# Moving the first branch's merge products into the attentions, and six more early gate units, in a two-block layer on one Trainium2 core

## The chip, the cores and the metric

The kernel runs on one core of a Trainium2 chip. The metric is the device time of one execution in microseconds. Before the change the median of three runs is 2440.82 us (2437.47 to 2442.12). The engines are TensorE (PE, its weight loads PEld), VectorE (DVE), ScalarE (ACT), GpSimd (POOL) and SyncE (SP), which here only issues transfers.

## What is computed

Two blocks over 512 tokens of width 1024, in float32. The first is attention and convolution with a mixture of experts (`peer_ffn`); the second has three branches that are gated and merged:

```python
h = rms_norm(x, norm_g)
p = h @ w_in
y_a = rwkv7_mix(...) * silu(z_a)                      # a recurrence over the tokens
y_b = sliding_window_sink_attn(q, k, v, pos, ...) * silu(z_b)   # q, k normalised, then rope
y_c = memory_cross_attn(xq, mem, ...) * silu(z_c)
gates = sigmoid(p_gate).reshape(b, t, 3, 1024)
merged = gates[..., 0, :] * (y_a @ w_proj_a) + gates[..., 1, :] * (y_b @ w_proj_b) \
       + gates[..., 2, :] * (y_c @ w_proj_c)
x = x + merged @ w_out
```

`rope` turns pairs that lie 32 apart in each head of 64: out = u * cos + crossed(u) * sin, where crossed(u) exchanges the two halves of 32 and changes one's sign. In the expert layer each token picks 16 of 16384 experts for each of 8 heads, by the best sums of two score lists; it takes a dot product with each picked row of `peer_u`, then adds up the picked rows of `peer_v` by weight.

## The kernel before

Activations of the projections lie transposed, with 128 channels on the partitions and the 512 tokens along the free dimension. All weights come in one stream of **units** of 128 x 1024 floats (512 KB) through a ring of four (`Weights`, L172). A product is made of three matmuls on parts rounded to fp32r (`product`, L165: high by high at L167, high by low at L168, low by high at L169); ScalarE makes the high part of each unit (`high_part`, L221 and L225, two buffers, made for unit u + 2 once TensorE finished unit u, `finished`, L229), GpSimd the low part (`low_parts`, L242), and VectorE does it in the expert stage (`low_part`, L250). The order of the units is `UNITS` (L68).

Much projection work is independent of what runs at its time and is laid beside other work by a **Filler** (L275): each `fill.pe(pe, n)` emits n steps on TensorE, ScalarE copies a finished unit to `stage` (L349), and SyncE stores it in `z_store` (L353). The second filler does the 46 units of `fill2`, each 128 channels of a projection: four for the gate of the recurrence, ten for the sliding attention (q, k, v and its gate), eight for the memory attention, and 24 for the sigmoid gates of the merge. A *whole* step is one `product` of 512 columns (three matmuls), eight to a unit.

**Early units.** 40 of the 46 units (`EARLY`, L67) are computed for their first 384 tokens beside the experts, in `merge_and_experts` (L1158), before the last 128 tokens exist. `early_steps` (L1108) spreads their steps, with those of 13 units for the recurrence, over the groups `Z_FROM` to `Z_UNTIL` (L1094 and L1095), that is 204 to 254. These steps have 384 columns, eight to a unit. SyncE loads each unit and stores 384 tokens of it. Later the filler makes only the last 128 tokens of these units, as a *short* step: two plain float32 matmuls at L320, four steps to a unit (`PART_STEPS`). Steps by stage before: 46 in `rwkv_prepare`, 89 in `rwkv_core`, 3 + 8 + 6 in `finish_branches`, 38 in `sliding_attention`, up to 21 in `memory_attention`. In all there are 40 x 4 + 6 x 8 = 208, so the last 30 of the sliding attention and 18 of the memory attention are whole ones.

**Experts.** A group is two picks of one head for a tile of 128 tokens: GpSimd issues two gathers (L1602), each 128 rows of 2048 floats (1 MB); VectorE makes the dot products (L1921), ScalarE the gelu (L1549) and the scaled diagonals (L1556), and TensorE adds the weighted rows with them (L2182). The four tiles come one after another. At its start, SyncE loads the rows of w_out (`raw_out`, a ring of four) and the query weights (`raw_query`, a ring of three) in plain float32 for the first tile: TensorE multiplies at L2137 (output product), then at L2082 (queries). The normalised tiles 1 to 3 of h2 lie over `raw_query`; VectorE writes them in the order 2, 3, 1 (`REST`, L998) by `scale` (L1838 to L1844), each waiting for the queries that read the slot beneath it: {1: 10, 2: 8, 3: 9}.

**finish_branches** (L3027) normalises y_a by head, gates it, normalises and turns q and k. q and k come back from `z_store` as `swz` in one transfer (L2995). Five matmuls by a signed permutation with the gain multiplied in (`swap`, L3055 to L3061) give crossed(u) in PSUM; `rotate` (L3144) on VectorE multiplies it by the sine (L3148), the straight part by gain and cosine (L3150), and adds (L3154). TensorE's order by hand: sums of y, swap 0 and 1, sums of squares of y, sums of squares of q and k (L2208), swap 2 and 3, three fill steps, spreads (L2217), sums for the memory queries, swap 4, v turned (L3093), eight fill steps, spreads, six fill steps. After it follow the two attentions (`attention`, L433) with fill steps in each iteration.

**merge_second** (L3257) runs twelve products, three branches for each of four pairs of output rows. Product n has 8 steps (4 for each of two rows), goes to bank pair n % 2 and waits for the gating of n - 2. SyncE loads the gates (512 KB for each n); ScalarE makes the sigmoid (L3313), VectorE multiplies bank by gate (L3356), adds the second and third branch to the first (L3361), and after the third splits the sum in high and low (L977 and L979). Eight units of w_out follow.

## Time and profile before

| | busy us | share of the span |
|---|---|---|
| profiled execution | 2434.74 (own time) | span 2432.9 |
| TensorE | 2159.3 | 89% |
| TensorE weight loads | 1445.3 | 59% |
| VectorE | 1762.3 | 72% |
| ScalarE | 852.9 | 35% |
| GpSimd | 701.1 | 29% |
| transfers | 713.53 MB, 293 GB/s mean | gathers 53.4% of 16 engines |

The stages lie so: first block up to about 450 us, the output product and the experts from 450 to 1933 us (first gathers at 497), recurrence 1933 to 2169, finishing the branches 2169 to 2219, sliding attention 2219 to 2276, memory attention 2277 to 2311, merge 2315 to 2384, the last product to the end. Durations in a timeline are those of one instruction or of a run of equal ones (x8: eight records; a plain float32 matmul has two records). "idle before <-" says how long the engine stood and who released it. The lower of TensorE's two clocks (1.2 GHz of 2.4) is a granted share of 0.50. A stage average says little about what ends last in it; the rows below are of single stages.

### The profile page before, as it was taken

How to read it: one execution, taken by the hardware profiler on the slowest of the kernel's cores; microseconds unless marked ns; L12 is line 12 of the kernel's file. 1: busy time of each engine (PE TensorE's matmuls, PEld its weight loads, DVE VectorE, ACT ScalarE, POOL GpSimd, SP SyncE). 2: the span in 40 equal slices, each digit the busy share in tenths (PEclk: the TensorE clock that was granted, in tenths of full speed). 3: DMA queues.
4: the chain of work that ended last, by engine and by line, in shares of the span. 5: the costliest groups of instructions: out<-in, count | busy, mean ns of one | idle time of the engine just before them, and what ended most of it. 6: DMA issues, size and time to landing. Idle time of an engine off the chain costs nothing. (4 is left out here: it accounts for less than half of the span.)

```text
span 2432.9 us, 34962 instructions
## 1 busy us (share of the span) xinstructions
PE 2159.3 (89%) x12602; PEld 1445.3 (59%) x12602; DVE 1762.3 (72%) x3986; ACT 852.9 (35%) x1969; POOL 701.1 (29%) x574
## 2 busy tenths in 40 slices
PE   8999899998999898877777888799999899888999
PEld 6887566664444444423233333377777788876777
DVE  7999696587666766677777767789887685456663
ACT  4222664143323323232333233333333332225631
POOL 0000312364333333334343333443334100001133
PEclk9999999999999999999999999999999999988999
DMA  4333214499999999999999999999999852342152
GB/s 155 104 104 113 75 52 154 176 377 415 421 413 421 419 418 416 413 417 400 421 419 420 417 413 409 411 404 418 421 421 421 318 170 82 117 160 82 60 187 95
DMA packets 137210, 713.53 MB, mean 293 GB/s; under 512 B 14672, under 2 KB 25296, under 8 KB 71248
## 3 DMA queue, kind: packets, MB, share of 16 engines
q0 software_dynamic: 73728, 536.90, 53.4%
q1 hardware_dynamic: 63312, 174.41, 20.0%
q8 instruction: 101, 1.65, 0.3%
q14 instruction: 69, 0.57, 0.1%
HBM read 689.76 MB, written 21.50 MB: 292 GB/s over the span
## 5 line engine op out<-in xcount | busy, mean ns | idle before, releaser
L2182 PE MATMUL bank<-peer_uv,peer_diag 128*128 128x512 f32 x1844 | 869.5, 614 | 202.1 <-ACT peer_diag L1556 200.8
L1921 DVE SCALAR_TENSOR_TENSOR peer_uv<-peer_uv,h 128x1024 f32<-128x1024 f32 x512 | 619.2, 1220 | 345.7 <-DMA peer_uv<-in_peer_uv,peer_index 345.3
L1602 POOL DMA_INDIRECT peer_uv<-in_peer_uv,peer_index x512 | 554.2, 1082 | 846.5 <-PE bank L2182 581.4
L2182 PEld LDWEIGHTS bank<-peer_uv,peer_diag 128*128 128x128 f32 x1844 | 338.6, 194 | 641.4 <-issue 640.6
L169 PE MATMUL bank<-hT_high,weight_low 128*128 128x384 f32 (+1 forms) x952 | 345.8, 363 | 0.0
L167 PE MATMUL bank<-hT_high,weight_high 128*128 128x512 f32 (+1 forms) x744 | 322.5, 434 | 5.6 <-POOL weight_low L250 2.3
L242 POOL TENSOR_TENSOR weight_low<-weight_ring,weight_high 128x1024 fp32r<-128x1024 f32 x46 | 112.1, 2437 | 611.2 <-ACT weight_high L225 611.2
L1549 ACT ACTIVATE peer_gelu<-peer_dots 128x2 f32<-128x2 f32 (+1 forms) x257 | 52.2, 203 | 644.9 <-DVE peer_uv L1921 644.5
L168 PE MATMUL bank<-hT_low,weight_high 128*128 128x512 f32 (+1 forms) x744 | 275.0, 370 | 0.0
L225 ACT ACTIVATE weight_high<-weight_ring 128x1024 fp32r<-128x1024 f32 x145 | 153.1, 1056 | 298.2 <-PE bank L169 271.9
L1556 ACT ACTIVATE peer_diag<-const,peer_weight 128x128 f32<-128x128 f32 x461 | 162.8, 395 | 234.0 <-DVE peer_weight L1717 233.7
L169 PEld LDWEIGHTS bank<-hT_high,weight_low 128*128 128x128 f32 x952 | 179.4, 188 | 18.2
L167 PEld LDWEIGHTS bank<-hT_high,weight_high 128*128 128x128 f32 x744 | 140.8, 189 | 48.7 <-issue 27.8
L168 PEld LDWEIGHTS bank<-hT_low,weight_high 128*128 128x128 f32 x744 | 140.9, 189 | 40.7 <-issue 25.6
L250 DVE TENSOR_TENSOR weight_low<-weight_ring,weight_high 128x1024 fp32r<-128x1024 f32 x89 | 108.6, 1220 | 10.1 <-ACT weight_high L225 10.1
L250 POOL TENSOR_TENSOR weight_low<-weight_ring,weight_high 128x1024 fp32r<-128x1024 f32 x10 | 34.3, 3434 | 261.8 <-ACT weight_high L225 261.7
L320 PE MATMUL bank<-last_h,weight_ring 128*128 128x128 f32 x640 | 89.6, 296 | 3.2 <-ACT fill_stage L349 3.2
L925 DVE SCALAR_TENSOR_TENSOR convT_whole<-z_u,cols,convT_whole 128x512 f32<-128x512 f32 x120 | 90.0, 750 | 0.0
L320 PEld LDWEIGHTS bank<-last_h,weight_ring 128*128 128x128 f32 x640 | 82.4, 207 | 9.2 <-issue 6.9
L925 DVE SCALAR_TENSOR_TENSOR z_odd<-z_u,cols,z_odd 128x512 f32<-128x512 f32 x112 | 84.0, 750 | 0.0
L167 PE MATMUL bank<-hT_high,early_high 128*128 128x384 f32 x208 | 79.8, 384 | 0.0
L168 PE MATMUL bank<-hT_low,early_high 128*128 128x384 f32 x208 | 70.4, 339 | 0.0
(469 smaller groups left out, 3160.7 us busy)
## 6 DMA issues: line engine op xcount, KB each, us to landing
weight_ring<-in_weights SPq DMA_DIRECT2D x224, 512.0 KB, 4.2
peer_uv<-in_peer_uv,peer_index POOLq DMA_INDIRECT x512, 10.5
z_store<-fill_stage SPq DMA_DIRECT2D x30, 256.0 KB, 2.4
z_store<-early_stage SPq DMA_DIRECT2D x40, 192.0 KB, 13.2
merge_z<-z_store SPq DMA_DIRECT2D x8, 768.0 KB, 6.6
merge_z<-z_store SPq DMA_DIRECT2D x12, 512.0 KB, 4.5
raw_query<-in_weights SPq DMA_DIRECT2D x10, 512.0 KB, 5.3
raw_out<-in_weights SPq DMA_DIRECT2D x8, 512.0 KB, 7.4
```

The costliest lines, as they stand in the source:

```text
L167: nc.tensor.matmul(to, left[0], right[0], start=start, stop=False)
L168: nc.tensor.matmul(to, left[0], right[1], start=False, stop=False)
L169: return nc.tensor.matmul(to, left[1], right[0], start=False, stop=stop)
L225: self.nc.scalar.activation(self.high_at(u).bitcast(F32R), self.ring[:, u % RING], ACT.Copy).then_inc(self.high_ready, 1)
L242: self.nc.gpsimd.tensor_tensor(self.low[:, slot].bitcast(F32R), self.ring[:, slot], self.high_at(u), ALU.subtract).then_inc(self.split, 1)
L250: vector.tensor_tensor(self.low[:, u % RING].bitcast(F32R), self.ring[:, u % RING], self.high_at(u), ALU.subtract).then_inc(self.split, 1)
L320: mm = self.nc.tensor.matmul(to, self.ring[:, f], self.last[:, f], start=f == 0, stop=f == DT - 1)
L925: nc.vector.scalar_tensor_tensor(to, u[:, c, k:k + T], cols("conv_w", k * DT + c), to, ALU.mult, ALU.add).then_inc(tap_done, 1)
L1556: nc.scalar.activation(diag[:, p % SLOTS], ident, ACT.Copy, scale=weight[:, p % TOPK:p % TOPK + 1]).then_inc(diag_ready, 1)
L1602: pool.indirect_dma_start(uv[:, p % SLOTS], None, peer_uv, bass.IndirectOffsetOnAxis(index[:, n % 2, p % TOPK:p % TOPK + 1], 0)).then_inc( ...
L1921: nc.vector.scalar_tensor_tensor(uv[:, p % SLOTS, 0:D], uv[:, p % SLOTS, 0:D], 1.0, h2[:, t], ALU.mult, ALU.mult, accum_out=dots[:, p % TO ...
L2182: mm = nc.tensor.matmul(bank[2 * t + c][:], diag[:, p % SLOTS], uv[:, p % SLOTS, D + c * 512:D + (c + 1) * 512], start=(n == first_of(t) a ...
```

## The change

1. `EARLY` is 46: all units of `fill2` have their first 384 tokens made beside the experts. The steps in the 50 groups grow from 408 to 456, and two low parts can fall into one group (`while lows`).
2. The products of the first branch (four of the twelve of the merge) become eight **half units** of the second filler: four whole steps each, two to a weight unit. They are stored ungated in rows 46 to 53 of `z_store`. The filler has 46 x 4 + 8 x 4 = 216 steps; 11 are left for the start of the merge. `merge_second` has 8 products, reloads the first branch (`first`, two buffers, 512 KB each) and gates it from SBUF. ScalarE's and SyncE's orders follow.
3. The swap products go. Four transfers of 32 partitions x 5 x 2 KB, issued behind that of `swz`, load the rows with the halves of 32 exchanged, and VectorE multiplies them by a signed gain and by the sine. Fill steps in the finish are 3 + 4 + 4.
4. `raw_out` has six slots, of which two lie in slots 0 and 1 of `raw_query`. The loads go in the order raw_out 4, 5, query 0, raw_out 6, 7, query 1, 2; the queries move one slot on, and `scale` waits for {1: 8, 2: 9, 3: 10}.

```diff
-EARLY = 40
+EARLY = 46
@@ Filler
-            self.begins.append(self.begins[-1] + (PART_STEPS if n < part else DT))
+            self.begins.append(self.begins[-1] + (PART_STEPS if n < part else DT if n < whole else DT // 2))
...
+            else:
+                e = (n - self.whole) % 2
+                mm = product(self.nc, to, self.ring[:, DT // 2 * e + k], self.items[n][0][:, k], k == 0, k == DT // 2 - 1)
+                if e == 0 and k == DT // 2 - 1:
+                    mm.then_inc(self.half_done, 1)
+                ends = e == 1 and k == DT // 2 - 1
@@ merge_and_experts, SyncE
                 w.load(sp, ub + RING)
                 sp.wait_ge(w.done, ub)
-                for m in range(3):
+                for k in (4, 5):
+                    raw_out_load(k)
+                raw_query_load(0)
+                for k in (6, 7):
+                    raw_out_load(k)
+                for m in (1, 2):
                     raw_query_load(m)
-                for k in range(4, DT):
-                    raw_out_load(k)
@@ merge_and_experts, VectorE
-                        dve.wait_ge(raw_query_done, {1: 10, 2: 8, 3: 9}[t])
+                        dve.wait_ge(raw_query_done, {1: 8, 2: 9, 3: 10}[t])
...
-                    if lows < LOWS_BESIDE and low_group(lows) <= g:
+                    while lows < LOWS_BESIDE and low_group(lows) <= g:
@@ second_block
-                  lambda n: first_unit("fill2") + n, [(hT, ACT.Copy, 1.0)] * FILL2, z_store, EARLY, places[1])
+                  lambda n: first_unit("fill2") + n if n < FILL2 else first_unit("merge") + (n - FILL2) // 2,
+                  [(hT, ACT.Copy, 1.0)] * FILL2 + [None] * (2 * FIRST_MERGED), z_store, EARLY,
+                  places[1], FILL2)
@@ rwkv_core, SyncE
                 sp.dma_start(late.swz[:], fill.store[4:14].rearrange("n p t -> p n t")).then_inc(swz_arrived, 16)
+                for o in range(0, P, 32):
+                    o2 = o + 32 if o % HD == 0 else o - 32
+                    sp.dma_start(late.crossed_z[o:o + 32], fill.store[4:9, o2:o2 + 32].rearrange("n p t -> p n t")
+                                 ).then_inc(crossed_arrived, 16)
@@ finish_branches, TensorE
-                pe.wait_ge(swz_arrived, 16)
-                swap(0)
-                swap(1)
...
-                swap(2)
-                swap(3)
                 fill.pe(pe, 3)
...
-                swap(4)
-                pe.wait_ge(crossed_ready, 4)
+                pe.wait_ge(swz_arrived, 16)
...
-                fill.pe(pe, 8)
+                fill.pe(pe, 4)
...
-                fill.pe(pe, 6)
+                fill.pe(pe, 4)
@@ finish_branches, VectorE
-                    nc.vector.tensor_tensor(crossed[:, i % 2], bank[4 + i % 2][:], sin, ALU.mult).then_inc(crossed_ready, 1)
+                    nc.vector.scalar_tensor_tensor(crossed[:, i % 2], late.crossed_z[:, i], late.cross_gain[:, i // 4:i // 4 + 1], sin,
+                                                   ALU.mult, ALU.mult).then_inc(crossed_ready, 1)
@@ merge_second
+    products = 12 - FIRST_MERGED
+    place = lambda m: 3 * (m // 2) + 1 + m % 2
...
-                fill.pe(pe, DT * FILL2)
-                for n in range(12):
-                    ring = w.wait(pe, u0 + n)
-                    if n >= 2:
-                        pe.wait_ge(parts, 2 * (n - 1))
+                fill.pe(pe, DT * fill.limit)
+                for m in range(products):
+                    ring = w.wait(pe, u0 + m)
+                    if m >= 2:
+                        pe.wait_ge(parts, 2 * (place(m - 2) + 1))
...
-                    if n >= 2:
-                        w.finished(act, u0 + n - 2)
+                    if n >= 4 and n % 3:
+                        w.finished(act, u0 + n - n // 3 - 3)
...
-                        nc.vector.tensor_tensor(to, bank[2 * (n % 2) + e][:], gate[:, n % 2, e], ALU.mult
+                        of = bank[2 * ((n - n // 3 - 1) % 2) + e][:] if n % 3 else first[:, n // 3 % 2, e]
+                        nc.vector.tensor_tensor(to, of, gate[:, n % 2, e], ALU.mult
```

## Rows read from the trace of the kernel before

**Rows 1.** Busy time by stage: stretch, length, five engines, granted clock, transfer share, GB/s.

```profile
1620.00:1680.00 60.00, 58.23 (x272) 47.58 (x271) 53.80 (x113) 21.98 (x42) 23.52 (x19) 1.00 1.02 419
...
2219.00:2276.00 57.00, 54.86 (x354) 38.21 (x354) 41.86 (x168) 41.30 (x129) 12.02 (x5) 0.94 0.25 84
...
2315.00:2384.00 69.00, 68.91 (x289) 55.57 (x290) 43.48 (x48) 25.70 (x24) 26.43 (x11) 0.98 0.51 176
```

**Rows 2.** DMA issues, 1600 to 1900 us: tensors, queue, count, KB each, us to landing.

```profile
z_store<-early_stage SPq DMA_DIRECT2D x33, 192.0 KB, 13.5
```

**Rows 3.** Timeline of TensorE, 1888 to 1898 us: start, duration, engine, line, operation, idle before.

```profile
1890.22 1.95 PE L2182 MATMUL bank<-peer_uv,peer_diag 128*128 128x512 f32 x4 [0.49 <-ACT peer_diag L1556]
...
1891.61 0.74 PE L167 MATMUL bank<-hT_high,early_high 128*128 128x384 f32 x1
...
1896.89 1.52 PE L2182 MATMUL bank<-peer_uv,peer_diag 128*128 128x512 f32 x3 [0.50 <-ACT peer_diag L1556]
```

**Rows 4.** Waits between 1600 and 1900 us: who waits for whom, us, times, longest.

```profile
DVE peer_uv L1921 <- DMA peer_uv<-in_peer_uv,peer_index: 45.9, 39, 2.8
```

**Rows 5.** Timelines of TensorE and SyncE's queue around 455 us.

```profile
453.32 7.03 PE L2137 MATMUL bank<-raw_out,merged_whole 128*128 128x512 f32 x16
...
463.94 8.83 PE L2137 MATMUL bank<-raw_out,merged_whole 128*128 128x512 f32 x16 [3.59 <-DMA raw_out<-in_weights]
...
455.31 5.40 SPq L1282 DMA_DIRECT2D raw_out<-in_weights  x4
```

**Rows 6.** Timelines of VectorE and GpSimd, 540 to 552 us.

```profile
540.12 1.28 DVE L1843 SCALAR_TENSOR_TENSOR h<-x,peer_rstd,rows 128x1024 f32<-128x1024 f32 x1
...
546.19 1.28 DVE L1843 SCALAR_TENSOR_TENSOR h<-x,peer_rstd,rows 128x1024 f32<-128x1024 f32 x1 [1.16 <-PE bank L2082]
...
551.64 1.63 POOL L1602 DMA_INDIRECT peer_uv<-in_peer_uv,peer_index  x1 [4.77 <-PE bank L2182]
```

**Rows 7.** Timeline of TensorE in the finish of the branches, 2166 to 2219 us.

```profile
2176.22 1.98 PE L3060 MATMUL bank<-swz,swap_gains 128*128 128x512 f32 x4 [1.70 <-DMA swz<-z_store]
...
2189.85 3.76 PE L3060 MATMUL bank<-swz,swap_gains 128*128 128x512 f32 x4
...
2204.80 3.27 PE L320 MATMUL bank<-last_h,weight_ring 128*128 128x128 f32 x24
```

**Rows 8.** Timeline of VectorE in the same stretch.

```profile
2190.03 0.20 DVE L3179 TENSOR_SCALAR finish_ms<-bank 128x40 f32<-128x40 f32 x1 [7.48 <-PE bank L2208]
```

**Rows 9.** Timeline of TensorE in the sliding attention, 2238 to 2242 us.

```profile
2238.72 0.70 PE L471 MATMUL bank<-swz 64*128 64x256 f32 x4
...
2240.35 0.48 PE L167 MATMUL bank<-hT_high,weight_high 128*128 128x512 f32 x1
...
2241.90 0.70 PE L471 MATMUL bank<-swz 64*128 64x256 f32 x4
```

**Rows 10.** Timelines of VectorE, ScalarE and GpSimd in the merge, 2328 to 2340 us.

```profile
2328.09 1.29 DVE L3356 TENSOR_TENSOR merge_part<-bank,merge_gate 128x512 f32<-128x512 f32 x2 [4.31 <-PE bank L169]
...
2329.30 3.42 DVE L3361 TENSOR_TENSOR merged2T_whole<-merged2T_whole,merge_part 128x512 f32<-128x512 f32 x2
...
2333.69 1.29 DVE L3356 TENSOR_TENSOR merge_part<-bank,merge_gate 128x512 f32<-128x512 f32 x2 [0.97 <-PE bank L169]
...
2338.24 0.41 DVE L977 CAST merged2T_high<-merged2T_whole 128x512 fp32r<-128x512 f32 x1
...
2338.69 0.69 DVE L979 TENSOR_TENSOR merged2T_low<-merged2T_whole,merged2T_high 128x512 fp32r<-128x512 f32 x1
...
2328.02 1.06 ACT L225 ACTIVATE weight_high<-weight_ring 128x1024 fp32r<-128x1024 f32 x1 [3.08 <-PE bank L169]
...
2329.16 2.41 POOL L242 TENSOR_TENSOR weight_low<-weight_ring,weight_high 128x1024 fp32r<-128x1024 f32 x1 [3.20 <-ACT weight_high L225]
```

**Rows 11.** The page's DMA issues, columns as in group 2.

```profile
z_store<-fill_stage SPq DMA_DIRECT2D x30, 256.0 KB, 2.4
...
merge_z<-z_store SPq DMA_DIRECT2D x12, 512.0 KB, 4.5
```

More of the change, by code:

```diff
@@ L3431, in constants @@
     halves = (p // 64 == c // 64)
[L3433 to L3438 removed]
+    sign = np.where(np.arange(P) % 64 < 32, -1.0, 1.0).astype(np.float32)[:, None]
     s2 = np.arange(2 * P)[None, :]
```

131 lines of the change are left out of this document (75 added, 56 removed).

## The prediction

> **What bounds the kernel now.** I read the busy time by stage first [rows 1]. Three kinds of stage matter here. In the experts, of which 1620 to 1680 us is a sample, the transfers run at a share of 1.02 and 419 GB/s while TensorE is busy 58.23 of 60 us: the DMA engines are full and TensorE is almost full too. The waits name the tighter one: VectorE stood 39 times for the expert rows, 45.9 us in all [rows 4], and TensorE's wait at a group of picks is 0.50 us [rows 3]. The groups repeat every 1896.89 - 1890.22 = 6.67 us [rows 3]. From 2166 us on the transfers are mostly light: finishing the branches (from 2166 to 2219), the sliding attention (57 us, TensorE busy 54.86) and the merge (69 us, busy 68.91) [rows 1] go by TensorE and by the chains that feed it. So a microsecond of TensorE is worth a microsecond in the merge and nearly that in the attention, a part of one in the finish, and nothing in the experts until it passes the transfers there.
>
> **1. Start of the experts.** Today eight matmuls' worth of output product waits 3.59 us for raw_out at 463.94, because the four last loads are issued at 455.31, after three query loads [rows 5]. With six slots two of the four go out first, and the two behind a single query load. The stall goes: 3.6 us, and up to 5.1 if the matmuls behind it, which take 8.83 us instead of 7.03 at the lower clock that follows the stall [rows 5], also recover 1.4 to 1.5. I take -5, since the loads are the only thing named; low end -3.6. What is late next is the merged input, which is ready in time for the first half.
>
> **2. The changed waits of scale.** scale(2) waits today for 8 queries and started at 540.12 without a wait; scale(3), which waits for 9, started at 546.19 after 1.16 us on TensorE [rows 6]. Now scale(2) waits for the ninth, so it moves to about 546.1, 6.0 us later. Queued behind it on VectorE are two dot products of a running group (1.22 us each) and the picks after them; who waits for those is TensorE, and behind it the gather on GpSimd, here the one at 551.64, itself after 4.77 us of waiting [rows 6]. Nothing in these rows is idle by itself, so of the 6.0 us some 4 reach the gathers, less what the one wait takes out of the next (1.16) and TensorE's own wait. I take +4, ends 0 and +6. A loss here shifts everything in the experts, as later groups are bound by transfers and do not catch up.
>
> **3. Six more early units in the experts.** Each loads 512 KB and stores 192 KB, a row of 384 tokens [rows 2]: 6 x (524,288 + 196,608) bytes = 4.33 MB. At the row's 419 GB/s [rows 1] that is 10.3 us if transfers stay the bound. TensorE gets 48 steps more in 50 groups, 0.96 a group, each of three 384-column matmuls; from 1891.61 to 1896.89, less the 0.50 of waiting, TensorE makes 24 of them and then has the next group, hence about 0.18 us each after the first and 0.5 us a group more [rows 3]. A group then needs 1896.89 - 1890.22 - 0.50 + 0.5 = 6.67 us of TensorE if its wait vanishes, against 6.67 + 0.206 = 6.88 us of transfers: the transfers still win, by 3%. But in 1620 to 1680 TensorE is at 58.23, and 9 groups x 0.5 makes 62.7 us against 61.9 of transfers; two resources that close do not overlap perfectly. I take +12, ends +9 and +20. The six low parts fall to VectorE, 1.2 us each, inside its 1.2 us waits for rows [rows 4].
>
> **4. Finishing the branches.** The five swap products go: two in 1.98 us, two in 3.76 us, which is the granted clock at 1.2 instead of 2.4 GHz, and the fifth in about 1.98 at that lower clock, 7.7 us of TensorE, and so does TensorE's wait of 1.70 us for swz [rows 7], since the first use of swz is now the sums of squares. Six fill steps leave: a step is 4 records, 24 of them take 3.27 [rows 7], so 6 x 0.545 = 3.3 us. Sum 12.7 us of TensorE. What is late next: the crossed loads, four of 0.33 MB issued behind swz (1.31 MB, 3.1 us at 419 GB/s), so VectorE begins the rotations nearer 2179.5 than 2177.4 and the mem and xqz loads behind them land 3 us later. VectorE had 7.48 us of waiting on the sums of squares [rows 8], which takes this. Following the order of TensorE and VectorE through, I end the stage about 2207 to 2208 instead of 2218: -10, ends -6 and -12.7. The two gain operations on [128, 1] and four more issues on SyncE's queue cost nothing, they lie in the scan, whose SyncE has no load due then.
>
> **5. The sliding attention.** Its iteration lasts 2241.90 - 2238.72 = 3.18 us [rows 9] and holds two whole fill steps, six 512-column matmuls, 1.55 us from 2240.35 to 2241.90 [rows 9]. All of its 38 steps are short ones now (4 x 46 = 184 short steps, of which 46 + 89 + 11 lie before), so these two become 8 records, 1.05 to 1.1 us [rows 7]: 0.47 us less in 15 iterations, 7 us, and 1.0 us of a wait for a low part goes. VectorE is busy 41.86 of 57 us [rows 1] and the row-by-row chain of maximum, exponential and sum takes over somewhere, so -6.5, ends -3 and -9.
>
> **6. The memory attention** has 21 whole steps instead of 18, over the same 0.70 us each, the three more in iterations that stood partly idle: +0.5, ends 0 and +2.
>
> **7. The merge.** Before: 12 products, each 5.60 us (2333.69 - 2328.09 between their first readers [rows 10]), 68.5 us with the slow first ones. After: 11 steps of fill (7.7 us, 9.1 with the low clock at the start), then 8 products, 44.8: TensorE alone would end at 53.9. But the first branch must be stored (2.4 us for 256 KB) and reloaded (4.5 us for 512 KB) [rows 11] after the last fill: 9.1 + about 1 + 2.4 + 4.5 + 1 of issue = 18. VectorE per pair of outputs: three gatings of 1.29, two additions of 3.42, two splits of 1.1, together 12.9 [rows 10], against 11.2 of TensorE. And the high part of the next weights stands on ScalarE behind the gate of two places on, then 1.06 and 2.41 us on GpSimd [rows 10]. Stepping through these: the third product starts at 25.8, the fifth at 39.0, the seventh at 51.4, and the eighth ends at 62.6. So -5.9; I take -5.5, ends -14.7 (TensorE alone) and 0.
>
> **Sum.** -5 + 4 + 12 - 10 - 6.5 + 0.5 - 5.5 = -10.5 us. The profiled execution took 2434.74, so 2424.2; the median of the three runs lies 6.1 us above it, so 2430.3 on the scale of the median. A measurement of this kernel can tell some 0.2% (4.9 us) from no change.
>
> **A rule that speaks against it.** The additions that read two operands from SBUF take 3.42 us for two, 1.71 each, the gatings that read PSUM and SBUF 0.65 each; GpSimd's low part of 2.41 us begins just before the additions [rows 10]. The eight gatings of the first branch will read two operands from SBUF as well. At 0.65 each step 7 stands; at 1.71 each they take 8 x 1.06 = 8.5 us more, which is rival B. The Trainium skill, "SBUF — State Buffer", section "Who interferes with whom", has a rule for it: a VectorE instruction with two SBUF inputs contends with a GpSimd instruction that reads SBUF, and whoever comes second waits for the whole of the other. The trace agrees with it in these rows. By the rule it costs only where a low part is under way when the gating comes; by my stepping-through the low parts end 2 us or more before, which is why it isn't the forecast.
>
> **Rivals.**
> A, slower: the experts become bound by TensorE's own order. Place: a group between Z_FROM and Z_UNTIL. TensorE's wait for peer_diag (0.50 us) is not slack but a loop from picks to weights, and stays; then a group lasts 6.67 + 0.5 = 7.17 to 7.25 us, 50 x 0.5 to 0.6 = 25 to 30 us instead of 12. For it: TensorE is at 58.23 of 60. Against it: VectorE's waits for rows, 45.9 us. It decides the sign from 7.2 us a group on: +27 there makes +5 in the sum. Time 2443 to 2450; I say 2448. Chance 0.12.
> B, within the measurement: the eight gatings of the first branch take 1.71 us as the additions do, 2.1 us more on VectorE in each pair; three pairs lie before the last product, so it ends at 62.6 + 6.3 = 68.9 and the merge lasts as before (+5.5); and the finish, with TensorE idle more often, spends its 9.7 us of sums and products at 1.2 GHz as the swap at 2189.85 does [rows 7], so that it gives only 5 (+5). Time 2441. Chance 0.16.
> C, the loads are hidden and TensorE is the only bound behind the experts: -12.7 - 9 - 14.7, with +9 for the experts and -5 at the start, is about -28: 2412 to 2416. Against it: the 18 us that the first branch needs in the merge. Chance 0.14.
> D, the change does only half: crossed loads come so late (they need the fill store's rows and SyncE) that the rotations set the finish. Then -4 instead of -10: 2436. Chance 0.10. The rest, 0.48, is the forecast with its own range of 2422 to 2439.
>
> **Chances.** Faster by over 0.2% (below 2435.9): 0.42 of the forecast's 0.48, 0.14 of C, 0.05 of D, 0.02 of B: 0.63. Within: 0.06 + 0.05 + 0.13 + 0.03 (A) = 0.27. Slower (above 2445.7): 0.09 of A, 0.01 of B: 0.10. The range goes from 2416 (C) to 2446, which leaves out half of A and half of C.
>
> **What the profile after would show.** Step 1: no wait for raw_out near 464. Step 2: a VectorE wait of about 6 us at 540 minus 5. Step 3: 6.9 us between gathers, share still 1.02; at 7.2 A holds. Step 4: no line for swap, about 43 us of stage. Step 5: iterations of 2.7 us. Step 7: TensorE idle up to 5 us ahead of every second product, waiting for a low part of GpSimd or for a gating, and eight first gatings of 0.65 us (B: 1.7). The prediction is wrong if groups of the experts pass 7.2 us, or if the three stages behind together give less than 10 us.

## The result and the profile after

Over 20 runs each, the changed kernel takes 2443.89 us (2438.94 to 2452.66) and the kernel before 2438.40 us; the ratio is 1.0031 with a 95% interval of 1.0021 to 1.0040 (two slow runs of the kernel before, 2665.53 and 3520.37 us, are left out of it). It is slower by 5.5 us by the medians and 7.6 us by the ratio, a small difference but clear of no change, where 10.5 us less were forecast. The two profiled executions lie 8.9 us apart (spans 2441.8 and 2432.9).

Where it went, read from the two traces. The first column runs from the first matmul of the output product to the first gather. The second and the third both start at that gather and run to those of group 10 and of group 206, so the third holds the second; the fourth runs from group 206 to 254 (48 groups). Then come the finish, from the last matmul of the scan (the recurrence) to the first of the sliding attention, that attention, the memory attention, and the merge, from its end to the first product with w_out:

| us | start | to g10 | to g206 | 206 to 254 | finish | sliding | memory | merge | span |
|---|---|---|---|---|---|---|---|---|---|
| before | 43.4 | 58.5 | 1085.4 | 314.9 | 49.9 | 58.0 | 34.9 | 72.0 | 2432.9 |
| after | 37.8 | 65.1 | 1091.1 | 340.1 | 48.2 | 51.6 | 35.1 | 68.0 | 2441.8 |
| forecast of the change | -5 | +4 | +4 | +12 | -10 | -6.5 | +0.5 | -5.5 | -10.5 |

Without the second column, which the third holds, these changes add up to +13.4 us against -10.5 forecast. The largest misses are the fourth column (13.2 us) and the finish (8.3 us). What is left (the first block, the scan) is the same code and still moved by up to 5 us between traces, so small differences are taken from repeated runs below.

The windows that answer to [rows 1] (start and end, length, five engines, granted clock, transfer share, GB/s):

```profile
1620.00:1680.00 60.00, 60.00 (x288) 50.74 (x287) 54.81 (x111) 23.02 (x44) 22.44 (x19) 1.00 1.01 414
...
1800.00:1860.00 60.00, 50.93 (x225) 41.05 (x226) 47.42 (x84) 21.21 (x40) 22.00 (x16) 0.93 0.96 382
...
2240.00:2289.00 49.00, 44.27 (x375) 33.81 (x373) 39.93 (x162) 34.59 (x123) 2.35 (x1) 0.99 0.36 114
...
2327.00:2392.00 65.00, 54.81 (x225) 42.86 (x225) 36.78 (x48) 24.21 (x25) 22.11 (x9) 0.95 0.62 219
```

TensorE is full in the first of them, then at 50.93 of 60 us, while the transfers fall to a share of 0.96 and 382 GB/s: neither is the bound there. The 48 groups as a whole, before and after:

```profile
1582.13:1897.04 314.91, 293.92 (x1346) 236.27 (x1347) 265.24 (x506) 113.13 (x216) 120.48 (x97) 1.00 1.01 417
```

```profile
1579.04:1919.14 340.10, 315.78 (x1470) 263.43 (x1471) 272.73 (x513) 119.72 (x228) 125.95 (x96) 0.97 1.00 400
```

The share of the transfer engines hardly moves (1.01 to 1.00), but the rate falls from 417 to 400 GB/s: a full share alone does not show that the stage moves its bytes as fast as before. The waits between 1600 and 1940 us say who stood. Before, VectorE stood for the low part of a weight unit for 2.6 us in all; after:

```profile
DVE weight_low L251 <- ACT weight_high L226: 33.0, 14, 5.4
...
DVE peer_uv L1947 <- DMA peer_uv<-in_peer_uv,peer_index: 23.3, 21, 2.4
...
DVE weight_low L251 <- ACT early_high L226: 11.7, 7, 6.5
```

One of these waits, in order of cause. SyncE issues the load of a unit at 1839.27; ScalarE, which splits the units in the order of their loads, gets it only at 1852.13; VectorE stands 5.45 us ahead of the low part at 1853.22; behind that stand its picks, so TensorE's diagonals and the next gathers come late:

```profile
1839.27 0.33 SPq L212 DMA_DIRECT2D weight_ring<-in_weights  x1
...
1852.13 1.06 ACT L226 ACTIVATE weight_high<-weight_ring 128x1024 fp32r<-128x1024 f32 x1 [3.17 <-DMA weight_ring<-in_weights]
...
1853.22 1.23 DVE L251 TENSOR_TENSOR weight_low<-weight_ring,weight_high 128x1024 fp32r<-128x1024 f32 x1 [5.45 <-ACT weight_high L226]
...
1856.36 3.75 PE L2208 MATMUL bank<-peer_uv,peer_diag 128*128 128x512 f32 x4 [4.24 <-ACT peer_diag L1582]
...
1856.42 1.31 POOL L1628 DMA_INDIRECT peer_uv<-in_peer_uv,peer_index  x1 [10.12 <-DVE x L1753]
```

GpSimd stood 10.12 us before it could issue, where 3 to 4 us are usual. What such a pause costs the transfers shows in the lower rate above.

At the start of the experts (TensorE, then VectorE and GpSimd, answering to [rows 5] and [rows 6]):

```profile
450.10 7.03 PE L2163 MATMUL bank<-raw_out,merged_whole 128*128 128x512 f32 x16
...
456.96 3.60 PE L2163 MATMUL bank<-raw_query,merged_whole 128*128 128x512 f32 x8
...
460.40 3.60 PE L2163 MATMUL bank<-raw_out,merged_whole 128*128 128x512 f32 x8
...
538.78 1.28 DVE L1869 SCALAR_TENSOR_TENSOR h<-x,peer_rstd,rows 128x1024 f32<-128x1024 f32 x1 [7.88 <-PE bank L2108]
...
487.94 1.09 POOL L1628 DMA_INDIRECT peer_uv<-in_peer_uv,peer_index  x1 [2.99 <-DVE peer_index L1722]
...
549.58 1.10 POOL L1628 DMA_INDIRECT peer_uv<-in_peer_uv,peer_index  x1 [10.19 <-PE bank L2208]
```

The stall of 3.59 us is gone. scale(2) now waits 7.88 us for the ninth query. The gather of group 9, which came 54.92 us after the first before (551.64 - 496.72), comes 61.64 us after it (549.58 - 487.94).

In the finish of the branches, answering to [rows 7], first the row of the kernel before that has the stage's first matmuls, then SyncE, TensorE and VectorE after:

```profile
2170.85 3.67 PE L3064 MATMUL bank<-yaT,const 128*128 128x512 f32 x8 [0.81 <-PEq L2546]
```


```profile
2188.20 0.38 SPq L3024 DMA_DIRECT2D swz<-z_store  x1
...
2188.62 4.26 SPq L3027 DMA_DIRECT2D crossed_z<-z_store  x4
...
2194.35 6.63 PE L3091 MATMUL bank<-yaT,const 128*128 128x512 f32 x8 [3.84 <-PEq L2575]
...
2201.76 13.77 PE L2234 MATMUL bank<-const,finish_sq 128*128 128x2 f32 x72 [0.78 <-DVE yaT L3180]
...
2206.65 0.75 DVE L3169 SCALAR_TENSOR_TENSOR crossed<-crossed_z,cross_gains,sincos 128x512 f32<-128x512 f32 x1 [4.94 <-DMA crossed_z<-z_store]
```

and the windows from 2190 to 2203:

```profile
2190.00:2197.00 7.00, 3.16 (x8) 1.49 (x7) 2.11 (x5) 0.92 (x3) 0.00 (x0) 0.75 0.98 360
...
2198.00:2203.00 5.00, 4.22 (x16) 2.14 (x15) 2.08 (x3) 2.52 (x5) 0.00 (x0) 0.77 1.07 207
```

SyncE issues the four crossed loads in 4.26 us, the larger swz in 0.38. The barrier between the blocks waits for it: TensorE's gap is 3.84 us instead of 0.81, and its first eight records take 6.63 us at 1.2 GHz where they took 3.67. From 2198 to 2203 the crossed loads are what is under way (nearly all bytes move in pieces of 2 KB, the length of their rows, and swz has landed by 2200.5): the transfer engines are busy (share 1.07), the rate is 207 GB/s, where it had been 360 with swz.

In the merge (VectorE's first gating, additions and casts, two of each; TensorE's three waits), answering to [rows 10]:

```profile
2345.86 1.29 DVE L3396 TENSOR_TENSOR merged2T_whole<-merge_first,merge_gate 128x512 f32<-128x512 f32 x2 [19.46 <-DMA merge_first<-z_store]
...
2348.28 1.28 DVE L3401 TENSOR_TENSOR merged2T_whole<-merged2T_whole,merge_part 128x512 f32<-128x512 f32 x2
...
2351.88 2.57 DVE L992 CAST merged2T_high<-merged2T_whole 128x512 fp32r<-128x512 f32 x1
...
2369.58 0.42 DVE L992 CAST merged2T_high<-merged2T_whole 128x512 fp32r<-128x512 f32 x1
...
2393.63 3.43 DVE L3401 TENSOR_TENSOR merged2T_whole<-merged2T_whole,merge_part 128x512 f32<-128x512 f32 x2
...
2354.22 0.79 PE L168 MATMUL bank<-ybT_high,weight_high 128*128 128x512 f32 x1 [8.13 <-POOL weight_low L243]
...
2367.48 0.50 PE L168 MATMUL bank<-ybT_high,weight_high 128*128 128x512 f32 x1 [0.40 <-POOL weight_low L243]
...
2380.87 0.50 PE L168 MATMUL bank<-ybT_high,weight_high 128*128 128x512 f32 x1 [1.63 <-POOL weight_low L243]
```

### The profile page after: what moved, and what is told of

Its sections match the earlier page's. It is cut to its first block and busy times, and to the rows that moved or that the text cites. A ratio compares the mean times of both kernels' runs of the same rounds, so it can differ in the third digit from the quotient of the medians.

```text
span 2441.8 us, 35192 instructions
## 1 busy us (share of the span) xinstructions
PE 2153.2 (88%) x12688; PEld 1455.1 (60%) x12688; DVE 1758.6 (72%) x3992; ACT 854.4 (35%) x1983; POOL 686.9 (28%) x568
## 5 line engine op out<-in xcount | busy, mean ns | idle before, releaser
L168 PE MATMUL bank<-hT_high,weight_high 128*128 128x512 f32 (+1 forms) x720 | 306.6, 426 | 4.5 <-POOL weight_low L251 2.3
L243 POOL TENSOR_TENSOR weight_low<-weight_ring,weight_high 128x1024 fp32r<-128x1024 f32 x40 | 98.1, 2454 | 608.9 <-ACT weight_high L226 608.9
L169 PE MATMUL bank<-hT_low,weight_high 128*128 128x512 f32 (+1 forms) x720 | 263.1, 365 | 0.0
L168 PEld LDWEIGHTS bank<-hT_high,weight_high 128*128 128x128 f32 x720 | 135.7, 188 | 45.9 <-issue 25.7
L169 PEld LDWEIGHTS bank<-hT_low,weight_high 128*128 128x128 f32 x720 | 135.7, 188 | 39.2 <-issue 24.9
L251 DVE TENSOR_TENSOR weight_low<-weight_ring,weight_high 128x1024 fp32r<-128x1024 f32 x92 | 112.1, 1219 | 43.4 <-ACT weight_high L226 43.1
L251 POOL TENSOR_TENSOR weight_low<-weight_ring,weight_high 128x1024 fp32r<-128x1024 f32 x10 | 34.3, 3435 | 258.5 <-ACT weight_high L226 258.4
L326 PE MATMUL bank<-last_h,weight_ring 128*128 128x128 f32 x736 | 99.1, 285 | 8.0 <-ACT fill_stage L364 4.5
L326 PEld LDWEIGHTS bank<-last_h,weight_ring 128*128 128x128 f32 x736 | 89.8, 196 | 13.4 <-issue 11.4
L168 PE MATMUL bank<-hT_high,early_high 128*128 128x384 f32 x232 | 90.8, 391 | 0.0
L169 PE MATMUL bank<-hT_low,early_high 128*128 128x384 f32 x232 | 79.3, 342 | 0.0
```

The lines of the kernel that those rows point to most:

```text
L168: nc.tensor.matmul(to, left[0], right[0], start=start, stop=False)
L169: nc.tensor.matmul(to, left[0], right[1], start=False, stop=False)
L243: self.nc.gpsimd.tensor_tensor(self.low[:, slot].bitcast(F32R), self.ring[:, slot], self.high_at(u), ALU.subtract).then_inc(self.split, 1)
L251: vector.tensor_tensor(self.low[:, u % RING].bitcast(F32R), self.ring[:, u % RING], self.high_at(u), ALU.subtract).then_inc(self.split, 1)
L326: mm = self.nc.tensor.matmul(to, self.ring[:, f], self.last[:, f], start=f == 0, stop=f == DT - 1)
```

## The experiments

All times are medians; each ratio is against runs of the kernel before that were taken with it, with its 95% interval. The kernel before itself had medians from 2433.77 to 2438.40 us in these sets, so kernels of different sets are compared by their ratios; "clear" means clear of the two intervals taken together, which is some 4 to 5 us. The stages are of one trace each and are read as in the table above.

| run | ratio to before | interval | to g10 | to g206 | 206 to 254 | finish |
|---|---|---|---|---|---|---|
| e1 loads as changed | 1.0006 | 0.9991 to 1.0021 | 66.0 | 1092.0 | 315.4 | 50.3 |
| e2 loads, old slots | 0.9977 | 0.9961 to 0.9992 | 58.4 | 1084.6 | 317.3 | 50.6 |
| e3 EARLY = 46 | 1.0047 | 1.0029 to 1.0065 | 59.9 | 1085.2 | 336.7 | 53.0 |
| e4 dense, EARLY = 40 | 1.0047 | 1.0027 to 1.0068 | 60.3 | 1087.3 | 324.9 | 52.7 |
| e5 as e3, two matmuls a step | 1.0006 | 0.9993 to 1.0019 | 59.8 | 1085.7 | 336.6 | 51.5 |
| e6 after, crossed loads later | 1.0019 | 1.0006 to 1.0032 | 63.1 | 1087.8 | 337.1 | 42.2 |
| e7 after, swaps kept | 1.0065 | 1.0052 to 1.0079 | 65.9 | 1090.7 | 340.4 | 54.8 |
| e8 after, EARLY = 40 | 1.0015 | 1.0001 to 1.0030 | 65.3 | 1091.1 | 316.1 | 43.0 |
| e9 as e3, splits a group later | 1.0035 | 1.0023 to 1.0048 | 58.3 | 1084.4 | 333.1 | 53.3 |
| e10 EARLY = 43 | 1.0023 | 1.0004 to 1.0041 | 59.9 | 1085.4 | 328.7 | 50.6 |
| e11 after, both repairs | 1.0011 | 1.0000 to 1.0023 | 58.2 | 1084.4 | 336.9 | 43.7 |
| e12 loads and crossed alone | 0.9968 | 0.9954 to 0.9982 | 58.5 | 1085.5 | 314.7 | 45.1 |
| e13 as e3, gathers a group later | 1.0084 | 1.0066 to 1.0102 | 58.6 | 1088.9 | 340.5 | 52.2 |
| e14 before, gathers a group later | 1.0064 | 1.0050 to 1.0077 | 59.8 | 1091.2 | 327.5 | 50.6 |

**The start of the experts: e1 and e2.** e1 is the fourth part of the change alone. e2 differs from it in this:

```diff
-                return raw_query[:, k - 4].rearrange("p k f -> p (k f)")
+                return raw_query[:, k - 3].rearrange("p k f -> p (k f)")
...
-                        dve.wait_ge(raw_query_done, {1: 8, 2: 9, 3: 10}[t])
+                        dve.wait_ge(raw_query_done, {1: 10, 2: 8, 3: 9}[t])
```

and the queries stay in slots m % 3.

> The kernel before with the fourth part of the change alone: six slots for raw_out, the two extra ones over slots 0 and 1 of raw_query, queries one slot on, scale waits {1: 8, 2: 9, 3: 10}. Theory L (the moved wait gives back most of what the earlier loads win): the first gathers start 8.8 us earlier, at 487.9 instead of 496.7; scale(2) then waits some 7 us for the ninth query and at the end of the experts only 3 us are left, so -3 us in all. Rival: the lead that is lost at scale(2) was lost to the other parts of the change; then this kernel is 8 to 9 us faster.

> As the run before, but the extra slots lie over slots 1 and 2 of raw_query, so that the queries keep their slots and scale its waits {1: 10, 2: 8, 3: 9}. Theory L: the 8.8 us of the start are kept through the experts, -8 us or so in all. Rival (the transfers are full from 500 us on, so an earlier start only moves the queue): -3 us, as the run before.

e1 took 2439.58 us, e2 2432.40, the kernel before 2437.83. From product to gather both need 37.9 and 37.8 us instead of 43.4. Every trace with the earlier loads has 37.8 to 38.0 us there, while the kernels without them have 40.5 to 44.1, so the loads are worth 3 to 6 us. The time of e2 is 5.6 us less than before by the ratio (2.0 to 9.5). Moving the waits of scale costs 7.2 us between the two medians, and by group 10 the traces are 7.6 us apart. The waits in question (e1, then e2):

```profile
539.51 1.28 DVE L1853 SCALAR_TENSOR_TENSOR h<-x,peer_rstd,rows 128x1024 f32<-128x1024 f32 x1 [6.19 <-PE bank L2092]
```

```profile
535.05 1.28 DVE L1853 SCALAR_TENSOR_TENSOR h<-x,peer_rstd,rows 128x1024 f32<-128x1024 f32 x1
...
541.12 1.28 DVE L1853 SCALAR_TENSOR_TENSOR h<-x,peer_rstd,rows 128x1024 f32<-128x1024 f32 x1 [0.87 <-PE bank L2092]
```

The rival of e1, that the lead was lost to the other parts of the change, falls: e1 is not faster than the kernel before. The -3 us expected for it was missed too, its interval ends at -2.2. Between theory and rival of e2 (-8 and -3 us) the time does not decide; the traces do: to group 206 e2 needs 1084.6 us from its first gather and the kernel before 1085.4, so full transfers did not swallow the earlier start.

**More early units: e3, e4, e5, e10.** e3 and e10 change `EARLY` alone, e4 the start of the early steps, e5 the step:

```diff
-Z_FROM = FINISH_AT[2] + 12
+Z_FROM = FINISH_AT[2] + 18
@@ e5, on top of EARLY = 46
-                            mm = product(nc, bank[2 + n % 4][:, 0:EARLY_T], ring[:, k], h3T[:, k, 0:EARLY_T], k == 0, k == DT - 1)
+                            to, left, right = bank[2 + n % 4][:, 0:EARLY_T], ring[:, k], h3T[:, k, 0:EARLY_T]
+                            nc.tensor.matmul(to, left[0], right[0], start=k == 0, stop=False)
+                            mm = nc.tensor.matmul(to, left[1], right[0], start=False, stop=k == DT - 1)
```

> The kernel before with EARLY = 46 alone (and the loop over the low parts that it needs). 48 more steps in 50 groups and 4.33 MB more. Theory S (weights arrive after the group in which ScalarE and VectorE are written to split them, and VectorE stands with the picks behind it): the experts last 20 to 25 us longer, with 20 us or more of VectorE waits at the low part, against some 5 us gained in the sliding attention and 4 where whole steps leave the memory attention: +12 to +18 us in all. Theory B (bytes): the experts last 10.3 us longer, and the total is within +0 to +3.

> The kernel before with EARLY = 40 as it was, but Z_FROM six groups later: the same 408 steps and the same bytes in 44 groups, 9.27 steps a group instead of 8.16. Theory B (bytes alone set the time): no change, 0 to +2 us. Theory S: the stalls at the low part appear without one byte more, 10 us or more longer. Theory T (TensorE has no room): a group needs 6.2 + 1.11 x 0.52 = 6.8 us against 6.65 of transfers in 44 groups, +6 us, and no waits at the low part.

> e3 (EARLY = 46 alone) with two matmuls in each early step instead of three: the product with the low part of the activations is left out there, so the gates and the z of the recurrence are less exact. Bytes, loads, their order and the places of the splits stay. A group has 9 x 0.175 = 1.6 us less of TensorE. Theory T (TensorE had no room): the experts come back to the 10.3 us of the bytes, without waits at the low part. Theory S (splits are written for a group in which the weights are not there yet): TensorE ends a unit a little earlier, so some waits go, but more than half of the 33 us of VectorE's waits at the low part stay, and the experts stay 15 us or more longer than before.

> The kernel before with EARLY = 43 alone: 8.64 steps a group, half of the way. Theory S as a threshold (a unit lasts 0.93 group, its successor in the ring is wanted 2.78 groups later): some waits at the low part, 10 to 20 us, and +5 us in all. Theory B: 5 us of bytes in the experts, +0 to +2 in all.

e3 took 2448.94 us, e4 2449.05, e10 2442.27, e5 2439.30. From group 206 to 254, e3 needs 21.8 us more than before, of which the bytes are 10.3 (an estimate, at 419 GB/s); e10 13.8, of which the bytes are 5.2; e4, without one byte more, 10.0. In time, e3 and e4 are both 11.5 us slower than before by the ratios, at the low end of what theory S had for e3 (+12 to +18). The waits at the low part appear in e4 as well as in e3. VectorE's waits from 1600 to 1940 us in e3, in e4 and in e5, and a window of e5:

```profile
DVE weight_low L250 <- ACT weight_high L225: 36.8, 15, 5.4
...
DVE weight_low L250 <- ACT early_high L225: 9.9, 5, 4.5
```

```profile
DVE weight_low L250 <- ACT weight_high L225: 25.6, 10, 5.4
...
DVE weight_low L250 <- ACT early_high L225: 11.7, 8, 5.4
```

```profile
DVE weight_low L250 <- ACT weight_high L225: 24.2, 10, 5.4
```

```profile
1800.00:1860.00 60.00, 42.31 (x164) 29.82 (x162) 45.53 (x82) 20.81 (x39) 20.36 (x16) 0.88 1.01 404
```

e4 falsifies the account by bytes alone. e5 falsifies the lack of room on TensorE: with 42.31 of 60 us busy it needs 336.6 us for the 48 groups, e3 336.7. The expectation for e5 was that some waits go and more than half stay; 26.8 us of 46.7 stayed, without any gain: VectorE waits 39.9 us for rows, in e3 21.7. Its better total is from other stages (from the end of the experts to that of the scan its trace is 7 us shorter) and is not explained. e10 shows that there is no threshold at 9 steps: at 8.64 VectorE already waits 30.7 us at the low part, where 10 to 20 were expected, and the groups cost 8.6 us over the bytes.

**What sets the waits: e9, e13, e14.**

```diff
@@ e9, on top of EARLY = 46
-KEEP_BEHIND = 2
+KEEP_BEHIND = 3
-    return Z_FROM + 1 + e - 2 if e < HIGHS else z_group(e - HIGHS) + 3
+    return Z_FROM + 1 + e - 2 if e < HIGHS else z_group(e - HIGHS) + 4
@@ e13 on top of EARLY = 46, e14 on the kernel before
-                        pool.wait_ge(summed, g - RINGS + 1)
+                        pool.wait_ge(summed, g - RINGS + 1 + (Z_FROM <= g < LAST_GROUP))
```

> e3 (EARLY = 46 alone) with ScalarE keeping unit n and splitting unit n + 4 three groups behind unit n's last step instead of two (KEEP_BEHIND = 3), and VectorE's low part four behind instead of three. Theory S, first form (the group was too early for the transfer, which lands 11 to 13 us after its issue): VectorE's waits at the low part fall from 47 us to under 10, and the kernel is 8 us or more faster than e3. Second form (a ring of four units is the limit: unit n + 4 is wanted by TensorE 2.6 groups after unit n's last step and now gets there after four): VectorE's waits go, TensorE waits for its weights instead, and the time is that of e3 or longer.

> e3 (EARLY = 46 alone) with each gather from group 204 on issued one group later (it waits for one more finished group of TensorE), so that up to 2 MB less stand in the queues in front of a weight load. Theory Q (latency of the weight loads behind the gathers sets the stalls): weights land some 3 to 5 us sooner, VectorE's waits at the low part fall from 47 us to under 20, and the experts get 5 to 10 us shorter than e3's. Theory R (the ring of four units and the order written for the engines): the waits at the low part stay above 35 us, and the kernel is as slow as e3 or slower, since expert rows come later too.

> The same gathers one group later in the kernel before, EARLY = 40: the control. Where the shorter lead costs nothing by itself, no change (within 2 us). If the lead was needed, VectorE's waits for expert rows grow from 50 us and the kernel is 5 us or more slower; then e13 has to be read against this.

e9 took 2443.12 us, 2.9 less than e3 by the ratios, which is not clear. Its waits (1600 to 1940 us):

```profile
POOL peer_uv L1602 <- PE bank L2182: 104.7, 25, 6.4
...
DVE weight_low L250 <- ACT weight_high L225: 18.3, 7, 5.3
...
PE bank L167 <- DVE weight_low L250: 14.7, 15, 2.5
...
DVE weight_low L250 <- ACT early_high L225: 5.0, 5, 1.7
```

VectorE's waits halve, and TensorE waits for its weights instead, and GpSimd for TensorE: between the two forms, nearer to the second. e13 and e14 change the gathers and leave the order of the splits alone. Where the gathers come one group later, the waits at the low part all but vanish:

```profile
DVE peer_uv L1921 <- DMA peer_uv<-in_peer_uv,peer_index: 64.5, 39, 3.7
...
DVE weight_low L250 <- ACT weight_high L225: 5.9, 5, 1.8
```

5.9 us instead of 46.7, as theory Q had it. Its other half failed: the 48 groups were to get 5 to 10 us shorter than in e3 and got 3.8 longer, as theory R said. The control shows why, since it needs 327.5 us for them instead of 314.9. Against its control e13 needs 13.0 us more, the bytes' 10.3 and 2.7 of stalls, where e3 needs 21.8 against the kernel before. So the stalls hang on how far the gathers run ahead, and the same lead is worth 12.6 us to the stage; e14 and e13 are 15.6 and 20.4 us slower than before. That each weight load landed sooner is not shown. With loads and splits paired in their order, a split for which ScalarE stood began 7.4 to 12.5 us after the issue of its load before (median 10.5), 7.3 to 13.2 in e3 (median 8.9) and 8.0 to 12.3 in e13 (median 10.1); between e3 and e13 what differs is how often it stood: 31 times of 44, and 12 of 45 (1620 to 1900 us). Before it stood 41 times of 43, which cost VectorE only 2.6 us. So the loads of e3 are not slower than those before; that they are needed earlier in the group is the account given below, and it is argued.

**Behind the experts: e6, e7, e8.** e6 moves the four issues from the end of `rwkv_core` to the start of SyncE's part in `finish_branches`:

```diff
@@ rwkv_core, SyncE
-                for o in range(0, P, 32):
-                    o2 = o + 32 if o % HD == 0 else o - 32
-                    sp.dma_start(late.crossed_z[o:o + 32], fill.store[4:9, o2:o2 + 32].rearrange("n p t -> p n t")
-                                 ).then_inc(crossed_arrived, 16)
@@ finish_branches, SyncE
+                for o in range(0, P, 32):
+                    o2 = o + 32 if o % HD == 0 else o - 32
+                    sp.dma_start(late.crossed_z[o:o + 32], fill.store[4:9, o2:o2 + 32].rearrange("n p t -> p n t")
+                                 ).then_inc(crossed_arrived, 16)
                 fill.wait_stored(sp)
```

e7 brings the swaps back (with 3 + 4 + 4 fill steps), e8 sets `EARLY = 40`.

> The changed kernel with the four crossed loads issued at the start of finish_branches instead of at the end of the scan. Theory Q (the 4.3 us in which SyncE issues them hold the barrier between the two blocks): TensorE's first matmul of the stage comes 3 us earlier, not at the lower clock; VectorE still waits for crossed_z, since its transfers are slow by themselves; 3 us faster in all. Rival (the loads are just late): they land 2 us later than now and the stage is as long or 2 us longer.

> The changed kernel with the third part undone (five swap matmuls, no crossed loads), its fill steps in the finish left at 3 + 4 + 4. By the two traces the third part gave 1.7 us in the stage, of which six fill steps fewer are 3.3; so without it: same to 2 us faster. If the crossed loads really save the 7.7 us of swaps, this kernel is 6 us or more slower than the changed one.

> The changed kernel with the first part undone (EARLY = 40), the rest as it is: 240 fill steps, 35 of them left at the start of the merge instead of 11. Experts 24 us shorter; sliding attention 6.4 us longer again; merge 24 x 0.70 = 17 us longer. Sum about -1 against the changed kernel, 2443. If it comes out under 2438, the parts behind the experts need no early gates to pay.

e6 took 2440.56 us, 2.9 less than the changed kernel by the ratios: the 3 us expected, but not clear (from 7 less to 1 more). TensorE's first records in the stage, VectorE's wait, and TensorE's first record of the sliding attention, then a window of VectorE's work between them, all of e6:

```profile
2194.56 3.67 PE L3087 MATMUL bank<-yaT,const 128*128 128x512 f32 x8 [0.82 <-PEq L2575]
...
2208.99 0.75 DVE L3165 SCALAR_TENSOR_TENSOR crossed<-crossed_z,cross_gains,sincos 128x512 f32<-128x512 f32 x1 [10.04 <-DMA crossed_z<-z_store]
...
2234.90 0.80 PE L486 MATMUL bank<-swz 64*128 64x128 f32 x4 [4.59 <-PEq L3083]
```

```profile
2209.00:2234.00 25.00, 20.61 (x179) 19.57 (x178) 22.70 (x45) 12.37 (x23) 0.00 (x0) 0.77 0.40 143
```

The gap is 0.82 us again and these records run at the full clock. The wait of 10.04 us takes the place of the 7.48 us for the sums of squares [rows 8], which are gone, but the lateness is not hidden: from 2209 us on VectorE is busy 22.70 of 25 us and never stands longer than 0.66 us for anyone, and TensorE stands 4.59 us ahead of the attention. VectorE's chain, which begins with the rotations when the crossed loads land, sets the end of the stage. e8 and e11 show the same: the attention begins 25.9, 26.7 and 25.1 us after VectorE's first rotation in e6, e8 and e11.

e8 also limits what e6 says. It issues its crossed loads at the end of the scan, as the changed kernel does, and its gap is 1.34 us at the full clock:

```profile
2169.96 3.67 PE L3091 MATMUL bank<-yaT,const 128*128 128x512 f32 x8 [1.34 <-PEq L2575]
```

Its four issues took 3.37 us and its finish 43.0 us, where the trace of the changed kernel has 48.2 with the same code. So the gap of 3.84 us and the slow clock behind it are of that trace, and it is not shown how often they come.

e7 took 2452.88 us, 8.3 more than the changed kernel by the ratios, and clear. My expectation, drawn from the two traces, was 0 to 2 us less and was wrong. This is the crossed loads against the swaps, with 3 + 4 + 4 fill steps in both. In the trace of e7 the first two swaps run at the lower clock (3.78 us, 1.98 before), and from 2210 to 2230 us the granted clock is 0.50; the finish takes 54.8 us, longer than before with six fill steps fewer. e8 took 2438.23 us, 3.9 less than the changed kernel by the ratios where 1 was expected, and not clear; 24.0 us of the experts come back, and the merge, with 35 steps of fill ahead of it, takes 82.1 us instead of 68.0.

**Together: e11 and e12.** e11 is the changed kernel with the edits of e2 and e6. e12 is the kernel before with the loads of e2, and with the crossed loads of e6 in place of the swaps; `EARLY`, the fill steps and the merge are as before.

> The changed kernel with two repairs: the extra raw_out slots over slots 1 and 2 of raw_query (queries and waits of scale as before), as in e2, and the crossed loads issued in finish_branches, as in e6. If both costs are what the runs say and add up: 7 + 3 = 10 us less than the changed kernel, 2434. The stalls at the low parts stay.

> The kernel before with what seems to pay, and nothing else: raw_out over slots 1 and 2 (e2) and the crossed loads issued in finish_branches in place of the swaps; EARLY = 40, fill steps 3 + 8 + 6 and the merge as before. e2 gave 5 us; in e6 the stage from the scan's end to the sliding attention took 42.2 us instead of 50, of which 3.3 are fill steps that here stay: 4 to 5 us. Sum 2427, faster than both kernels. If the swaps were hidden by something else, 2432 as e2.

e11 took 2437.20 us, 4.9 less than the changed kernel by the ratios, and clear, where 10 were expected. e12 took 2426.41 us (2419.51 to 2436.60): 0.32% faster than the kernel before and, by the two ratios, 0.6% faster than the changed one, the best version found, and as expected (2427). Its finish takes 45.1 us with all 17 fill steps, 4.8 less than before. In time it is only 2.2 us faster than e2, which is not clear.

## Why the prediction was wrong

The direction was wrong: 10.5 us less were forecast and 5.5 to 7.6 more were measured. By the two traces step 3 was short by 13.2 us, step 4 by 8.3, step 2 by 1.7 to 2.6 and step 7 by 1.5. Steps 2, 3 and 4 share one omission: a wait and a transfer were priced by their own length and rate, not by who stands in line behind them.

**Step 1** (-5) held: -5.6 in the changed kernel and -5.4 to -5.6 in e1, e2 and e12 against the trace of before, 3 to 6 us against all traces without the earlier loads.

**Step 2** (+4, ends 0 and +6) was too low: 6.6 us in the traces of before and after, and 7.2 by the medians of e1 and e2. The step that failed is "some 4 reach the gathers". The rows had said that nothing between scale(2) and the gather was idle, and most or all of the wait reaches them. The wait itself was 6.19 us in e1, e6 and e7, close to the 6.0 of the forecast, and 7.88 and 7.76 in the changed kernel and e8; group 10 came 4.6 to 7.5 us later in these five traces.

**Step 3** (+12, ends +9 and +20) is the main error: 25.2 us. The step that failed is "the transfers still win, by 3%", with some 2 us for imperfect overlap: the comparison of two rates decided nothing, and the stalls of VectorE at the low part (44.7 us in the changed kernel, 2.6 before) were put at nothing ("the six low parts fall to VectorE ... inside its 1.2 us waits for rows"). The 10.3 us of the bytes stand as an estimate. What was missing is the due time of each weight load. A unit is loaded when TensorE has finished the one four before it, and is split two groups later on ScalarE and three on VectorE. At 8.16 steps a group a unit lasts 0.98 of a group, so its end keeps its place in the group for long; at 9.12 it lasts 0.88 and moves through the group, and every eighth unit or so ends late in it. Then less than two groups, some 13 us, are left for a load that takes up to 12.5 us before and 13.2 in e3, and VectorE, ScalarE and the gathers behind them stand. That the waits come with the steps in a group, without one byte more (e4) and with TensorE far from full (e5), and go when the gathers come later (e13), is shown. That the moving place in the group is what starts each stall is argued from the order written in the code and from one such chain in the trace; no run took it alone.

**Rival A** had the number (25 to 30 us, 7.09 measured a group against 7.17 to 7.25) and not the mechanism. It put the loop in TensorE's wait for peer_diag; e5 shows 336.6 us, as long as e3, with TensorE far from full. That its range of 2443 to 2450 holds the measured time is luck; its own +27 makes +4.5 in the sum, which is 2445 and not 2448. Its chance of 0.12 was too small: the windows had shown two resources within 3% of each other, and only their rates were compared.

**Step 4** (-10, ends -6 and -12.7) missed in the trace of the changed kernel: the finish took 48.2 us instead of 49.9, 1.7 less. The same code gave 43.0 in e8, and with the later issues 42.2 in e6 and 43.7 in e11, which is 6 to 8 us less and inside the ends, but not -10. The prediction had the stage go by TensorE; behind the landing of the crossed loads it went by VectorE. The swap products did go, but what they are worth alone is not settled: 8.3 us by e7, 4.8 us of finish in e12, 2.2 us between e2 and e12. Two terms failed. "Four more issues on SyncE's queue cost nothing": in the changed kernel's trace they hold the barrier 3.0 us longer, with a stretch at 1.2 GHz behind it; in e8 the gap was only 0.5 us longer than before. And "VectorE had 7.48 us of waiting on the sums of squares, which takes this": the crossed loads do not come 3.1 us behind swz. They took 12.2 to 15.2 us to land, at 207 GB/s they ran at half of the rate I had used, and VectorE began its rotations 17.2 us after the end of the scan's last matmul, where it was 8.4 before and 10.5 by the forecast. The Trainium skill, "SBUF — State Buffer", section "Door 1: The DMA port swizzle", states that a range of 32 partitions reaches 8 of the 16 ports that transfers write through, and gives 189 to 218 GB/s for it. The trace agrees (207 GB/s). By the page's figures 1.31 MB would have been an estimate of 6.0 to 6.9 us. The row's 207 GB/s gives 6.3. It was overlooked. Rival D, that the crossed loads come so late that the rotations set the finish, named the place rightly, and e6, e8 and e11 show it; its reason (the fill store's rows and SyncE) was not this one, and its -4 lies between the changed kernel's trace and these three.

**Step 5** (-6.5) and **step 6** (+0.5) held: -6.4 and +0.2.

**Step 7** (-5.5): -4.0 from the end of the attention. From the stage's first matmul at 2326.95 the third, fifth and seventh product began after 27.3, 40.5 and 53.9 us where 25.8, 39.0 and 51.4 were stepped through, and the eighth ended after 65.4 and not 62.6. The order was right: the third product was 1.5 us late, the pair from it to the fifth took the 13.2 us forecast, the next 13.4 instead of 12.4. The gating of the first branch came 18.9 us after that matmul, where 18 were forecast. What was priced too low are the splits of the sum: the cast and the subtraction of one split take 0.42 and 0.69 us alone, as forecast, but 2.57 and 2.74 at 2351.88 and 2354.48, where GpSimd's low parts run beside them. Rival B did not come: in all four pairs two gatings of the first branch took 1.28 or 1.29 us, and no low part ran beside them. Two additions took 1.28 us where none ran and 3.43 where one did, which is the contention that rival B feared, in the place where it was already; so 1.71 us for each, as in the prediction, is one wait spread over two.

## What to carry to other kernels

A transfer needs two prices, its bytes at the stage's rate and its latency in that stage's queue against the distance at which its reader was written; where a fixed order reads it "two groups later", check that distance again whenever the rate of work per group changes. An instruction on an in-order engine that waits costs everything queued behind it: where nothing between it and the bound resource is idle, take the whole wait and not a share. And look at what ends a block: issues on the emptiest queue can hold the barrier (a gap of 3.84 us in one trace, 1.34 in another of the same code), and behind the longer gap the clock was the lower one as well. A saving on one engine ends where the next engine's chain begins: here the swaps left TensorE, and the chain that begins with VectorE's rotations set the stage.

## What the runs showed of the hardware

Four loads of 32 partitions (320 KB each, rows of 2 KB) moved 207 GB/s at a transfer share of 1.07, where the load of 128 partitions ahead of them had run at 360 GB/s and more; so a full share with a low rate is how such loads look. Four such issues took SyncE 4.26 us in the changed kernel and 1.78 to 3.37 us in e6, e8, e11 and e12, against 0.38 us for one of 2560 KB. In the experts' stage, one group of gathers less in flight (2 MB) took VectorE's waits for weights from 46.7 to 5.9 us (e3, e13) and yet made 48 groups of the kernel before 12.6 us longer (e14). VectorE's cast of 128x512 took 0.42 us alone and 2.57 us beside a low part on GpSimd.
